# Two transformer blocks on one core: order of the first outputs, lead of the weight splits, places of the waits, and row pitch of two operands

## The chip, the cores and the metric

The kernel is one program on one core of one Trainium2 chip. The metric is its device time in microseconds (us), lower is better. Before the change it takes 1228.34 us, the median of three runs (1228.14 to 1228.73).

## The reference

Everything is float32, one sequence of S = 256 tokens, width D = 1024. Written short:

```
block 1: x += 0.5*swiglu(norm(x), gate0, up0, down0)            # D_FF 2816
         q,k,v,g = norm(x) @ w_in                               # 5888 columns: 12 dilated-window heads, 8 MoBA heads, 2 gates
         x += (sigmoid(ga)*(y_a @ w_up_a) + sigmoid(gb)*(y_b @ w_up_b)) @ w_out
         x += 0.5*swiglu(norm(x), gate1, up1, down1);  x = norm(x)
block 2: (sh, sc, g) x 4 = silu(c) @ ada_w + ada_b              # modulation
         layer 0: x += g1*sliding_window_sink_attention(h(x));  x += g2*swiglu(h(x), gate2, up2, down2)
         layer 1: x += g1*stick_breaking_attention(h(x));       x += g2*swiglu(h(x), gate3, up3, down3)
norm(x) = x * rsqrt(mean(x*x) + 1e-6) * gain;   h(x) = norm(x)*(1+sc) + sh
```

(w_in has 3*768 + 3*512 + 2*1024 columns.) The work is almost all weight matmuls: 2992 weight tiles of 128x128, each against the 256 tokens.

## The kernel before, in words

**Data.** x lies transposed, as KD = 8 slices of 128 features by 256 tokens. To keep float32 accuracy every operand is split in a high and a low part of a reduced float32 format: a weight w into `whi` and `wlo`, the normed input h into `hhi` and `hlo` (8 slices, k = 0..7), the hidden of a swiglu into `hidhi` and `hidlo` (22 slices). Each weight tile takes three matmuls of 256 columns: whi with hhi (L471), whi with hlo (L472), wlo with hhi (L475). Where the input has a shift (mix2, ffn2, mix3, ffn3), two more columns carry it: 258 columns. A row of `hhi` and `hlo` has S + 2 elements (1032 bytes), one of `hidhi` and `hidlo` 256 (1024 bytes).

**Stages.** In order: ffn0, down0, mix1, up, wout, ffn1, down1, mix2, wo2, ffn2, down2, mix3, wo3, ffn3, down3. `TILES` lists all tiles in order; 8 of them are a chunk of 512 KB (374 chunks), and the time that TensorE takes for one chunk is called a tick. "Tick 5.4" of a stage is tile 4 of its chunk 5. `by_output(outs, K, group, late)` sets a stage's order: the first `group` outputs do all k but the last `late` one after another, then the last k together; the rest go output by output. `heads_order` does it for wo2 and wo3, with k from LATE = 5 on left to the end.

**Queues.** SyncE loads chunks into 6 raw buffers (and 96 rows of `ada`, 512 KB each, between them). ScalarE (ACT) copies a chunk to `whi` (L1517, `hi(upto)`), VectorE (DVE) subtracts to `wlo` (L958, `lo(upto)`); both have rings of RING = 7. In tick t of a stage DVE makes `lo` up to chunk t + 2 and ACT `hi` up to t + 3. DVE also makes the modulation from `ada` (L964). Every engine works strictly in the order of the code, which is written by tick: the small operations of a tick stand before or after its `lo` or `hi`.

**Norms.** A stage doesn't wait for its norm: it multiplies raw x by the gain, and the result is scaled later by Rb, the reciprocal root of the mean square. ACT squares x (`squares`), GpSimd (POOL) adds the 8 slices (L1903), TensorE adds over partitions (`sums`, L501), DVE and ACT make the root (`variance`, `estimate`, `inverse`), TensorE spreads it (`spread`, L509), ACT copies it to Rb (`roots`, L1560).

**Residuals.** DVE adds a finished output m to x (`residual`, L984), then ACT makes hhi[m] (`operand_hi`, L1533) and DVE hlo[m] (`operand_lo`, L975) for the next stage. DOWN_AT, WOUT_AT and WO2_AT say in which tick; what is missing there comes after the loop.

**Attention.** TensorE does the head work between weight tiles: `scores`, transposes of the probabilities (`keys_first`, L560), products with v (`outputs`, L567). In mix1 `SETS` and `PAIRS` give the tick of each group of heads; `turns(jp, tick)` begins with `e.wait_ge(norm1, ...)`, ahead of its first `upto(tick, ...)`. mix2 (rotary keys, sinks) goes through one pair of heads a tick, mix3 one in three ticks; there `behind` (L897) does the cumulative sum, after DVE's and ACT's softplus.

Of the kernel before, what the change touches and what calls it, by code (L numbers as in the profile page):

```python
# [28 lines left out]
LATE = 5  # L29
# [34 lines left out]
def mix1_order():  # L64
    order = by_output(MIX1_OUTS[:6], KD, 3, 1)
# [14 lines left out]
def heads_order(name):  # L80

    order = [((name, m), k) for k in range(LATE) for m in range(KD - 2)]
    order += [((name, m), k) for k in range(LATE) for m in (KD - 2, KD - 1)]
# [140 lines left out]
def two_blocks(nc: bass.Bass, x_in, stream, ada, con_in, c_in, pos_in, out):  # L224
    with ExitStack() as ctx:
# [13 lines left out]
        hhi = sb("hhi", [P, KD, S + 2], F32R)  # L239
        hlo = sb("hlo", [P, KD, S + 2], F32R)  # L240
# [161 lines left out]
        def _(e):  # L402
# [5 lines left out]
            for s, (kind, n) in enumerate(SEQ):  # L408
# [35 lines left out]
        def _(e):  # L444
# [67 lines left out]
            def ffn(n):  # L512
# [4 lines left out]
                def begin(o, new):  # L517
                    w, f = o
                    up = w[0] == "u"
                    if new:  # L520
# [4 lines left out]
                        if n > 1 and f < 2:  # L525
# [45 lines left out]
            def mix1():  # L571
# [56 lines left out]
                def turns(jp, tick):  # L628
                    e.wait_ge(norm1, 2 * jp + 2)
# [15 lines left out]
                upto(3, 2)  # L645
# [80 lines left out]
            def mix2():  # L726
# [84 lines left out]
                upto(3, 2)  # L811
# [29 lines left out]
            def mix3():  # L841
# [104 lines left out]
        def _(e):  # L946
# [1076 lines left out]
```

## Time and profile before

| | us |
|---|---|
| median of 3 runs | 1228.34 |
| time of the profiled execution | 1227.34 |
| its span (first to last instruction) | 1225.4 |
| TensorE matmul busy (9696 matmuls) | 1181.0 (96%) |
| DVE busy | 905.2 (74%) |
| ACT busy | 637.2 (52%) |
| POOL busy | 106.9 (9%) |
| DMA | 251.92 MB, 206 GB/s mean |

Matmuls are pipelined, so the busy time of one (279 to 291 ns) overlaps the next; a matmul's price is the distance from start to start. Times are of one profiled execution; "idle before" is how long an engine stood before an instruction, with what released it.

### The profile page before, as it was taken

What the parts mean: (1) busy time and instruction counts of PE and PEld (TensorE: products, weight loads), DVE (VectorE), ACT (ScalarE), POOL (GpSimd) and SP (SyncE); (2) the same over time, 40 slices, a digit from 0 to 9 for tenths busy, and PEclk for the clock granted to TensorE, in tenths of its full rate; (3) what the DMA queues carried; (4) which work ended last, traced back from release to release, by engine and by line L of the source; (5) the groups of instructions that cost most, each with busy time, mean ns of one, the idle gap of its engine ahead of it and who ended that gap; (6) DMA issues with size and microseconds to landing.
All of it is one profiled execution on the core that took longest, in us unless ns stands there. A gap on an engine that the chain in (4) does not pass through costs nothing.

```text
span 1225.4 us, 23733 instructions
## 1 busy us (share of the span) xinstructions
PE 1181.0 (96%) x9696; PEld 1149.3 (94%) x9696; DVE 905.2 (74%) x1589; ACT 637.2 (52%) x1053; POOL 106.9 (9%) x146
## 2 busy tenths in 40 slices
PE   6999999988999999999999999999999998999999
PEld 5999999977889999999987889999998888999999
DVE  4689988465367899997979778888657777666643
ACT  5554555434464654444656654545447785544541
POOL 1000002022100100000455210000100001000000
PEclk8999999989999999999999989999999999999999
DMA  6597878542236588989742357778653434565552
GB/s 247 180 316 250 316 301 311 187 155 82 91 121 180 184 297 302 310 305 347 268 142 74 104 172 259 260 257 299 230 166 113 138 121 146 167 190 187 176 187 86
DMA packets 70524, 251.92 MB, mean 206 GB/s; under 512 B 7824, under 2 KB 9616, under 8 KB 70416
## 3 DMA queue, kind: packets, MB, share of 16 engines
q1 hardware_dynamic: 70416, 250.41, 61.0%
q8 instruction: 77, 1.26, 0.4%
q14 instruction: 31, 0.25, 0.1%
HBM read 249.33 MB, written 1.05 MB: 204 GB/s over the span
## 4 chain that ended last, share of the span: by engine, by line
PE 83%; DVE 11%; ACT 2%; issue 2%; POOL 1%; DMA 1%; SPq 0%; POOLq 0%; DVEq 0%; ACTq 0%
PE ps L471 25%; PE ps L475 25%; PE ps L472 25%; DVE wlo L958 2%; PE ps L567 1%; PE ps L462 1%; ACT s L1747 1%; PE ps L560 1%; PE ps L465 1%; PE ps L466 1%; DVE hlo L975 1%; PE ps L601 1%; DMA raw<-w_stream 1%; PE ps L897 1%; DVE s L1349 1%
## 5 line engine op out<-in xcount | busy, mean ns | idle before, releaser
L471 PE MATMUL ps<-hhi,whi 128*128 128x256 f32 (+1 forms) x1968 | 568.1, 289 | 7.2 <-DVE hlo L975 6.2
L475 PE MATMUL ps<-hhi,wlo 128*128 128x256 f32 (+1 forms) x1968 | 558.2, 284 | 1.0 <-DVE wlo L958 0.8
L472 PE MATMUL ps<-hlo,whi 128*128 128x256 f32 (+1 forms) x1968 | 557.8, 283 | 0.0
L958 DVE TENSOR_TENSOR wlo<-raw,whi 128x1024 fp32r<-128x1024 f32 x373 | 454.3, 1223 | 23.9 <-ACT whi L1517 23.2
L1517 ACT ACTIVATE whi<-raw 128x1024 fp32r<-128x1024 f32 x373 | 386.1, 1048 | 61.6 <-DMA raw<-w_stream 39.3
L471 PEld LDWEIGHTS ps<-hhi,whi 128*128 128x128 f32 x1968 | 374.7, 190 | 15.6 <-issue 14.3
L475 PEld LDWEIGHTS ps<-hhi,wlo 128*128 128x128 f32 x1968 | 374.8, 190 | 1.7 <-DVE wlo L958 1.3
L472 PEld LDWEIGHTS ps<-hlo,whi 128*128 128x128 f32 x1968 | 375.7, 191 | 0.3
L475 PE MATMUL ps<-hidhi,wlo 128*128 128x256 f32 x704 | 196.1, 279 | 0.0
L471 PE MATMUL ps<-hidhi,whi 128*128 128x256 f32 x704 | 196.1, 279 | 0.0
L472 PE MATMUL ps<-hidlo,whi 128*128 128x256 f32 x704 | 196.1, 279 | 0.0
L471 PEld LDWEIGHTS ps<-hidhi,whi 128*128 128x128 f32 x704 | 133.6, 190 | 0.0
L472 PEld LDWEIGHTS ps<-hidlo,whi 128*128 128x128 f32 x704 | 132.1, 188 | 0.0
L475 PEld LDWEIGHTS ps<-hidhi,wlo 128*128 128x128 f32 x704 | 132.1, 188 | 0.0
L964 DVE CUSTOM_DVE_ANT_0 raw<-raw,cond,vx 128x1024 f32<-128x1024 f32 x96 | 126.6, 1319 | 0.0
L1903 POOL TENSOR_TENSOR ss<-sq,ss 128x256 f32<-128x256 f32 x56 | 47.3, 851 | 792.8 <-ACT sq L1540 790.0
L1060 DVE TENSOR_TENSOR gu<-ps,Rb 128x512 f32<-128x512 f32 x88 | 60.4, 686 | 30.5 <-PE ps L475 30.4
L1573 ACT ACTIVATE sg<-gu,bcol 128x256 f32<-128x256 f32 x44 | 22.4, 510 | 105.7 <-DVE gu L1060 105.7
L1577 ACT ACTIVATE hidhi<-hidf 128x256 fp32r<-128x256 f32 x88 | 36.7, 419 | 47.0 <-DVE hidf L1068 33.0
L1573 ACT ACTIVATE sg<-gu 128x256 f32<-128x256 f32 x44 | 18.4, 418 | 80.3 <-DVE gu L1060 80.3
L1059 DVE COPY bcol<-ps 128x2 f32<-128x2 f32 x44 | 7.0, 160 | 61.5 <-PE ps L475 61.4
L984 DVE SCALAR_TENSOR_TENSOR vx<-ps,mod,vx 128x256 f32<-128x256 f32 x32 | 14.0, 477 | 49.1 <-PE ps L475 49.1
(216 smaller groups left out, 1257.1 us busy)
## 6 DMA issues: line engine op xcount, KB each, us to landing
raw<-w_stream SPq DMA_DIRECT2D x373, 512.0 KB, 4.5
raw<-ada_in SPq DMA_DIRECT2D x96, 512.0 KB, 4.8
out_dram<-vx SPq DMA_DIRECT2D x8, 128.0 KB, 2.4
con<-con_in SPq DMA_DIRECT2D x1, 962.0 KB, 6.1
raw<-w_stream SPq DMA_DIRECT2D x2, 256.0 KB, 3.4
vx<-x_in SPq DMA_DIRECT2D x2, 256.0 KB, 6.2
cond<-c_in SPq DMA_DIRECT2D x1, 512.0 KB, 4.4
vx<-x_in SPq DMA_DIRECT2D x3, 128.0 KB, 4.1
```

The source lines that it names most:

```text
L462: e.matmul(b, x_hi, wh, start=kt == 0 and tt == 0, stop=False, skip_group_check=True)
L471: e.matmul(bank, wh, r_hi, start=i == FIRST[o] and not shared, stop=False, skip_group_check=True)
L472: e.matmul(bank, wh, r_lo, start=False, stop=False, skip_group_check=True)
L475: mm = e.matmul(bank, wl, r_hi, start=False, stop=i == LAST[o], skip_group_check=True)
L958: e.tensor_tensor(wlo[:, n % RING, :], raw[:, slot, :], whi[:, n % RING, :].bitcast(F32), ALU.subtract).then_inc(lo_done, 1)
L964: e.tensor_tensor_reduce(raw[:, slot, :], raw[:, slot, :], cond[:], 1.0, v("adab", n), ALU.mult, ALU.add, mod[:, layer, j:j + 1]).then_inc ...
L984: e.scalar_tensor_tensor(x[:, m, :], ps[:, b, o:o + S], coef(r, m), x[:, m, :], ALU.mult, ALU.add).then_inc(x_new, 1)
L1060: e.tensor_tensor(gu[:, b, :, :], ps[:, p:p + 2, 0:S], Rb[:].unsqueeze(1).to_broadcast([P, 2, S]), ALU.mult).then_inc(gu_scaled, 1)
L1517: e.activation(whi[:, n % RING, :], raw[:, s % RAW, :], ACT.Copy).then_inc(hi_done, 1)
L1573: e.activation(sg[:, b, :], gu[:, b, 0, :], ACT.Silu, bias=bcol[:, b, 0:1] if n > 1 else 0.0).then_inc(sg_done, 1)
L1577: e.activation(hidhi[:, f, :], hidf[:, f % 3, :], ACT.Copy).then_inc(hid_hi, 1)
L1903: e.tensor_tensor(ss[:, i, :], sq[:, i, m % 2, :], ss[:, i, :], ALU.add).then_inc(ss_done, 1)
```

## The change

Eight edits in one diff:

1. `by_output` is called with late = KD in all stages: the first 3 or 4 outputs go k by k together. `heads_order` goes over k 0..2, then 3..5 (LATE = 6), each for outputs 0..3 and then 4..7; k = 6 and 7 come last, output by output.
2. `lo` runs to t + 3 (was t + 2) and `hi` to t + 4 (was t + 3) in all stages.
3. Norms: in the swiglu stages `sums` at tick 2.4 (was 1.4) and `spread` at 4.0 (was 3.2), in ffn0 at 5.0 and 6.4; `inverse` stands right behind `variance`, ahead of `lo`. In the mixers `spread` is at 2.4. In ffn0 ACT makes squares 3 to 7 between its first splits. `SCALE_AT` gives the ticks in which gate and up are scaled.
4. mix1: `turns` first runs `upto(tick)`, then waits, and starts 3 ticks after the scores (was 2); the second set and the pairs start 1 to 2 ticks later; the pair scores go ahead of the pair's turns. BIASES is 4 (was 5).
5. mix2: the key's root and `keys` stand ahead of `lo`. mix3: `outputs`, `behind` and `turn_values` come 3 to 4 tiles later.
6. wo2 and wo3: one pair of outputs is added in tick 7, the other three pairs after the loop, each with its own operands and squares.
7. Banks: FFN_OFF (0, 2, 2, 2) and down1, down2, down3 in bank m. ffn2 waits for 2 residuals instead of up to 8.
8. Rows of hhi, hlo, hidhi and hidlo are HS = S + 16 elements, 1088 bytes. x parts 3 to 5 are loaded one chunk later, behind chunks 1 to 3.

```diff
-LATE = 5
+LATE = 6
+HS = S + 16
-    return by_output(outs, KD, 4, 1 if n else KD)
+    return by_output(outs, KD, 4, KD)
...
-    order = [((name, m), k) for k in range(LATE) for m in range(KD - 2)]
-    order += [((name, m), k) for k in range(LATE) for m in (KD - 2, KD - 1)]
+    halves = range(0, KD // 2), range(KD // 2, KD)
+    order = [((name, m), k) for ks in (range(0, 3), range(3, LATE)) for half in halves for k in ks for m in half]
     return order + [((name, m), k) for m in range(KD) for k in range(LATE, KD)]
...
-SETS = [(17, 0, 0), (19, 0, 1), (23, 1, 0), (25, 1, 1)]
-PAIRS = [(29, 0), (31, 1), (33, 2), (35, 3)]
-BIASES = 5
+SETS = [(17, 0, 0), (19, 0, 1), (24, 1, 0), (26, 1, 1)]
+PAIRS = [(31, 0), (33, 1), (35, 2), (37, 3)]
+BIASES = 4
-WO2_AT = {6: (0, 1), 7: (2, 3)}
+WO2_AT = {7: (0, 1)}
-FFN_OFF = (0, 2, 0, 0)
+FFN_OFF = (0, 2, 2, 2)
+SCALE_AT = [{**first, **{t: (t // 2 - 1,) for t in range(10, 44, 2)}} for first in ({7: (0, 1), 8: (2,), 9: (3,)}, {5: (0, 1), 6: (2,), 8: (3,)})]
...
-        hhi = sb("hhi", [P, KD, S + 2], F32R)
-        hlo = sb("hlo", [P, KD, S + 2], F32R)
+        hhi = sb("hhi", [P, KD, HS], F32R)
+        hlo = sb("hlo", [P, KD, HS], F32R)
-            hidhi = sb("hidhi", [P, KF, S], F32R, scope)
-            hidlo = sb("hidlo", [P, KF, S], F32R, scope)
+            hidhi = sb("hidhi", [P, KF, HS], F32R, scope)[:, :, 0:S]
+            hidlo = sb("hidlo", [P, KF, HS], F32R, scope)[:, :, 0:S]
...
-                if s < 3:
-                    load_x(s + 3)
-                if s == 3:
+                if 0 < s < 4:
+                    load_x(s + 2)
+                if s == 4:
...  ffn on TensorE
-                            taken = ((4, 6), (8, 8))[f][up] if n == 2 else ((2, 4), (6, 8))[f][up]
-                            e.wait_ge(x_new, (s - 1) * KD + taken)
+                            e.wait_ge(x_new, (s - 1) * KD + 2)
-                tiles(c0 + CH + 4, begin, operand)
+                tiles(c0 + (2 * CH + 4 if n else 5 * CH), begin, operand)
                 sums(s)
-                tiles(c0 + 3 * CH + 2, begin, operand)
+                tiles(c0 + (4 * CH if n else 6 * CH + 4), begin, operand)
                 spread(s)
...  mix1 on TensorE
                 def turns(jp, tick):
+                    upto(tick)
                     e.wait_ge(norm1, 2 * jp + 2)
...
-                        turns(jp, tick + 2)
+                        turns(jp, tick + 3)
...
+                    pair_scores(p)
                     if p:
-                        pair_turns(p - 1, upto, keys_first, outputs, tick)
-                    pair_scores(p)
-                upto(37)
-                pair_turns(3, upto, keys_first, outputs, 37)
+                        pair_turns(p - 1, upto, keys_first, outputs, tick, 3)
+                pair_turns(3, upto, keys_first, outputs, 39, 6)
...  mix3 on TensorE
-                        upto(3 * i + 1, 6)
+                        upto(3 * i + 2, 2)
                         outputs(i - 2)
-                        upto(3 * i + 3, 2)
+                        upto(3 * i + 3, 6)
                         behind(i - 1)
-                        upto(3 * i + 3, 4)
+                        upto(3 * i + 3, 7)
                         turn_values(i)
...  DVE, every stage (ACT alike, + 3 to + 4)
-                    lo(c0 + t + 2)
+                    lo(c0 + t + 3)
...  DVE, mix2
+                    if t == 5:
+                        keys()
+                    if t == 4:
+                        roots(0, stk, None)
+                        key_roots()
-                    lo(c0 + t + 2)
-                    if t == 4:
-                        roots(0, stk, None)
-                        key_roots()
-                    if t == 5:
-                        keys()
+                    lo(c0 + t + 3)
-                residuals(3, (4, 5, 6, 7), c0 + 20)
+                for ms in ((2, 3), (4, 5), (6, 7)):
+                    residuals(3, ms, c0 + 20)
+                lo(c0 + 21)
...  ACT, ffn0
-            for m in range(KD):
+            for m in range(3):
                 squares(0, m)
+                    if n == 0 and t < 3:
+                        for m in ((3,), (4, 5), (6, 7))[t]:
+                            squares(0, m)
```

## Rows read from the trace of the kernel before

**Rows 1.** Page: busy time of each engine.

```profile
PE 1181.0 (96%) x9696; PEld 1149.3 (94%) x9696; DVE 905.2 (74%) x1589; ACT 637.2 (52%) x1053; POOL 106.9 (9%) x146
```

**Rows 2.** Waits of TensorE: engine, line, releaser, us in total, times, longest.

```profile
PE ps L462 <- DVE sA L1192: 9.9, 2, 5.0
PE ps L501 <- POOL ss L1903: 8.3, 1, 8.3
PE ps L471 <- DVE hlo L975: 6.2, 4, 3.0
PE ps L897 <- DVE zr L1435: 3.7, 7, 1.0
PE ps L560 <- DVE s L1349: 2.4, 2, 1.8
PE ps L763 <- DVE kT L1326: 2.1, 1, 2.1
PE ps L560 <- ACT vt L1802: 1.3, 1, 1.3
PE ps L471 <- DVE o2lo L1354: 1.0, 1, 1.0
PE ps L471 <- ACT mghi L1700: 1.0, 1, 1.0
```

**Rows 3.** Windows over the half-clock stretches: us, busy (x) PE, PEld, DVE, ACT, POOL, clock.

```profile
16.40:26.70 10.30, 5.59 (x26) 5.59 (x27) 3.30 (x8) 4.91 (x9) 3.94 (x6) 0.50 0.49 186
269.00:275.90 6.90, 4.69 (x22) 4.69 (x23) 3.10 (x5) 1.49 (x3) 3.83 (x3) 0.51 0.53 154
303.10:310.00 6.90, 4.38 (x20) 4.38 (x21) 3.41 (x5) 1.81 (x3) 4.15 (x3) 0.51 0.46 152
709.30:716.20 6.90, 6.09 (x27) 5.79 (x27) 4.43 (x5) 2.73 (x4) 2.58 (x4) 0.51 0.43 131
1033.60:1037.10 3.50, 3.29 (x16) 3.04 (x16) 2.38 (x3) 1.56 (x2) 0.82 (x2) 0.51 0.11 42
```

**Rows 4.** Windows, L471 alone: us, PE busy (xtiles), PEld; ffn1, down1, down2, ffn3.

```profile
440.00:540.00 100.00, 78.69 (x281) 52.81 (x280) 1.00 0.88 300
552.00:611.80 59.80, 48.54 (x176) 32.92 (x176) 1.00 0.85 306
838.70:900.80 62.10, 49.40 (x176) 33.72 (x176) 1.00 0.74 258
1080.00:1160.00 80.00, 62.87 (x224) 42.07 (x224) 1.00 0.58 184
```

**Rows 5.** Timeline of ACT and POOL at the start: start, us, what.

```profile
19.35 0.42 ACT L1540 ACTIVATE sq<-vx 128x256 f32<-128x256 f32 x1 [0.45 <-POOL ss L1903]
14.70 6.36 POOL L1903 TENSOR_TENSOR ss<-sq,ss 128x256 f32<-128x256 f32 x7 [14.27 <-ACT sq L1540]
```

**Rows 6.** Windows of all engines, columns as rows 3: middle of mix2, and ffn1.

```profile
672.00:678.00 6.00, 6.00 (x51) 5.12 (x50) 5.55 (x22) 3.95 (x13) 4.89 (x8) 1.00 0.27 79
425.20:552.00 126.80, 126.80 (x1065) 126.75 (x1064) 116.08 (x174) 62.81 (x93) 1.16 (x2) 1.00 0.88 300
```

**Rows 7.** Timeline of DVE from the end of wo2 into ffn2.

```profile
701.36 1.36 DVE L975 SCALAR_TENSOR_TENSOR hlo<-vx,gmod,hhi 128x256 fp32r<-128x256 f32 x2
704.57 1.83 DVE L975 SCALAR_TENSOR_TENSOR hlo<-vx,gmod,hhi 128x256 fp32r<-128x256 f32 x2
706.32 1.65 DVE L984 SCALAR_TENSOR_TENSOR vx<-ps,mod,vx 128x256 f32<-128x256 f32 x4
707.89 1.21 DVE L958 TENSOR_TENSOR wlo<-raw,whi 128x1024 fp32r<-128x1024 f32 x1
709.02 3.58 DVE L975 SCALAR_TENSOR_TENSOR hlo<-vx,gmod,hhi 128x256 fp32r<-128x256 f32 x4
```

**Rows 8.** Timeline of POOL over the same stretch.

```profile
708.92 3.40 POOL L1903 TENSOR_TENSOR ss<-sq,ss 128x256 f32<-128x256 f32 x4 [2.80 <-ACT sq L1540]
```

**Rows 9.** Groups of L471 by form: xcount, busy us, mean ns, idle before.

```profile
L471 PE MATMUL ps<-hhi,whi 128*128 128x256 f32 x992 | 284.4, 287 | 1.0 <-ACT whi L1517 1.0
L471 PE MATMUL ps<-hhi,whi 128*128 128x258 f32 x976 | 283.7, 291 | 6.2 <-DVE hlo L975 6.2
L471 PE MATMUL ps<-hidhi,whi 128*128 128x256 f32 x704 | 196.1, 279 | 0.0
```

More of the change, by code:

```diff
@@ L80, in heads_order @@
 def heads_order(name):
-    order = [((name, m), k) for k in range(LATE) for m in range(KD - 2)]
-    order += [((name, m), k) for k in range(LATE) for m in (KD - 2, KD - 1)]
+    halves = range(0, KD // 2), range(KD // 2, KD)
+    order = [((name, m), k) for ks in (range(0, 3), range(3, LATE)) for half in halves for k in ks for m in half]
     return order + [((name, m), k) for m in range(KD) for k in range(LATE, KD)]
 STAGES = (("ffn0", ffn_order(0)), ("down0", down_order(0)), ("mix1", mix1_order()), ("up", up_order()),
-          ("wout", by_output([("wout", m) for m in range(KD)], KD, 4, 1)),
-          ("ffn1", ffn_order(1)), ("down1", down_order(1)), ("mix2", by_output(MIX2_OUTS, KD, 3, 1)), ("wo2", heads_order("wo2")),
-          ("ffn2", ffn_order(2)), ("down2", down_order(2)), ("mix3", by_output(MIX3_OUTS, KD, 3, 1)), ("wo3", heads_order("wo3")),
+          ("wout", by_output([("wout", m) for m in range(KD)], KD, 4, KD)),
+          ("ffn1", ffn_order(1)), ("down1", down_order(1)), ("mix2", by_output(MIX2_OUTS, KD, 3, KD)), ("wo2", heads_order("wo2")),
+          ("ffn2", ffn_order(2)), ("down2", down_order(2)), ("mix3", by_output(MIX3_OUTS, KD, 3, KD)), ("wo3", heads_order("wo3")),
           ("ffn3", ffn_order(3)), ("down3", down_order(3)))
@@ L665, in pair_turns @@
                 for hh in range(2):
-                    upto(tick, 2 * hh)
+                    upto(tick, tile + 2 * hh)
                     keys_first(12 + 2 * p + hh, sA[:, hh, p % 2, :])
-                upto(tick, 4)
+                upto(tick, tile + 4)
                 outputs(6 + p, 6 + p, 12 + 2 * p + 2, True, True)
@@ L731, in begin @@
                     n = MIX2_OUTS.index(o)
-                    if new and n in (0, 1):
-                        e.wait_ge(x_new, 2 * KD + n + 1)
+                    if new and n < 3:
+                        e.wait_ge(x_new, 2 * KD + (1, 2, 6)[n])
                     if new and n == 5:
@@ L1239, in mix1 @@
                             normed(q, hh)
-                        if hh and t == tick + 4:
+                        if hh and t == tick + 5:
                             heads_lo(jp)
@@ L1476, in mix3 @@
                         shift_lo(3)
-                residuals(5, (4, 5, 6, 7), c0 + 34)
+                for ms in ((2, 3), (4, 5), (6, 7)):
+                    residuals(5, ms, c0 + 34)
+                lo(c0 + 35)
             e.memset(dg[:], 0.0).then_inc(zeroed, 1)
@@ L1667, in mix1 @@
                     for q, (tick, jp, hh) in enumerate(SETS):
-                        if hh and t == tick + 2:
+                        if hh and t == tick + 3:
                             for n in range(4):
                                 turned(6 * jp + n)
-                        if hh and t == tick + 3:
+                        if hh and t == tick + 4:
                             for n in range(4, 6):
@@ L1674, in mix1 @@
                             heads_hi(jp, 3 * jp + 3)
[L1675 to L1681 removed]
+                    hi(c0 + t + 4)
+                    if t == 2:
                         roots(1)
@@ L1686, in mix1 @@
                     for tick, p in PAIRS:
+                        if t == tick + 2:
+                            turned(12 + 2 * p)
+                            turned(12 + 2 * p + 1)
+                    for tick, p in PAIRS:
                         if t == tick:
                             pair_exps(p)
+                        if t == tick + 2:
+                            heads_hi(2 + p, 6 + p + 1)
                     if t == 40:
@@ L1790, in mix2 @@
                         operands(4, WO2_AT[t - 10])
-                operands(4, (4, 5, 6, 7))
-                hi(c0 + 21)
+                for ms in ((2, 3), (4, 5), (6, 7)):
+                    operands(4, ms)
+                hi(c0 + 22)
             def mix3():
@@ L1859, in mix3 @@
                         operands(6, WO2_AT[t - 24])
-                operands(6, (4, 5, 6, 7))
-                hi(c0 + 35)
+                for ms in ((2, 3), (4, 5), (6, 7)):
+                    operands(6, ms)
+                hi(c0 + 36)
             exp_ln_table()
```

121 lines of the change are left out of this document (57 added, 64 removed).

## The prediction, before the result was known

> **What bounds the kernel now.** I read the page's busy times first. TensorE is busy 1181.0 of 1225.4 us, DVE 74%, ACT 52%, POOL 9% [rows 1]. So time goes only where TensorE stands still, runs at the lower clock, or needs less for a matmul. Three views price these: its waits, the windows with a granted clock near 0.5, and windows in which only L471 is counted, one per weight tile.
>
> Standing still: the waits listed come to 36 us, of which 24.4 us are three places: two waits for mix1's probabilities (9.9), one for POOL's sum at the start (8.3), four for hlo (6.2) [rows 2].
>
> Lower clock: after five of these waits the granted clock is 0.5 (1.2 GHz) for a stretch. Work in it takes double. TensorE is busy in them 5.59, 4.69, 4.38, 6.09 and 3.29 us; half of it is lost: 2.8, 2.3, 2.2, 3.0 and 1.6 us, together 12.0 [rows 3].
>
> Price of a tile (three matmuls) at full clock, window by count: 100.0 / 281 = 0.356 us in ffn1 (256 columns), 80.0 / 224 = 0.357 in ffn3 (258 columns), 59.8 / 176 = 0.340 in down1, 62.1 / 176 = 0.353 in down2 [rows 4]. down1 and down2 read the same rows of the same tensors, and still there are two levels, 113 and 118 ns a matmul. No row says what picks one.
>
> **The change part by part.** The sum is made against the profiled execution, 1227.34 us; the median of the runs is 1.0 above it.
>
> *Start (edits 3 and 8).* The wait of 8.3 us ended at 21.1, when POOL's seven adds were done (14.70 + 6.36) [rows 2, 5]. TensorE had stopped at 12.8, after 12 tiles. Now `sums` stands at tile 40, so 28 tiles of 0.357, 10.0 us, lie ahead of it: 22.8. ACT's squares 3 to 7 now have splits of 1.05 us between them, which I let push the last add by about 1 us, to 22: covered, just. x parts behind the chunks make the first operands later; I charge 0.7. DVE's `variance` blocks no `lo` needed: chunks up to 7 are split ahead of it. The wait goes, and with it the low-clock stretch: 8.3 + 2.8 - 1.1 = 10.0. Bounds: 6 (the sum 4 us later) and 11.
>
> *mix1 (edit 4).* TensorE waits for norm1 right behind the scores, though 16 tiles that don't need it come next in its own queue; behind the wait stood everything. The wait now comes after 24 tiles, 8.6 us, more than the 5.0 us of each wait [rows 2]. Gone: 9.9, and 4.5 of low clock. The pairs' waits were small. BIASES 4 makes POOL write two of the second set's three biases only after the first set is softened; the 5.7 us between the sets (16 tiles) hide two adds of POOL's size (0.9 each [rows 5]). Without that cover it would cost 2. I take 14.5, bounds 10 and 15.5.
>
> *wo2 to ffn2, wo3 to ffn3 (edits 1, 6, 7).* Output by output, ffn2 wanted hlo of k = 4 at its fifth tile, 1.4 us in. k by k over four outputs it is wanted after 16 tiles, 5.7 us. DVE's work for a pair of slices: two residuals (1.65 / 4 = 0.41 each) and two hlo (3.58 / 4 = 0.90 each), 2.6 us [rows 7]. TensorE wants a pair each 8 tiles, 2.9 us. From the start of the tail of 16 tiles: first pair finished at 1.4, one split 1.2, four pairs 10.5, so the last at 13.1; wanted at 5.7 + 24 x 0.357 = 14.3. It holds with 1.2 to spare. What is late next: `sums` at tile 20, 12.8, wants the last add of POOL, about 14: 1.2 us in each stage. The next `wlo` (1.21) ends at 14.3, just as chunk 3 is wanted. Gone: 6.2 waits and 4.6 low clock, and 1.0 for o2lo, since k = 7 now comes 7 tiles behind its product. 11.8 - 2.4 = 9.4, bounds 4 and 12. New early use of outputs 4 to 7's banks adds a wait on `du2` in wo2 (TensorE alone stands behind it, under 1 us; inside the bounds).
>
> The hlo of those rows is slow when POOL adds: 1.36 for two while POOL has nothing, 3.58 for four during its four adds [rows 7, 8]. The Trainium skill, "SBUF — State Buffer", section "Who interferes with whom", says that a DVE instruction with two SBUF inputs and a GpSimd one that reads SBUF exclude each other. The trace agrees (0.68 and 0.90 us each). It speaks against edit 6, which puts POOL's adds among all pairs; I have used the slow value for all eight slices. By the fast one the tail would have 1.8 us more room, and the sum stays.
>
> *mix3 (edit 5).* `behind` waited 3.7 us in seven places, at most 1.0; it comes 4 tiles, 1.4 us, later. The transpose of v waited 1.3 and comes 3 tiles later [rows 2]. I take 4.5 of 5.0. `outputs` is moved by as much, and its users have 13 tiles. Bounds 2 and 5.
>
> *mix2 (edit 5), wout (edit 1).* The wait for kT, 2.1, shrinks, as a `lo` (1.21 [rows 7]) no longer stands before it. But in the middle of mix2 DVE is busy 5.55 of 6.0 us [rows 6], so what TensorE gains early it waits for later; the 2.4 us for s stay. 1.5, bounds 0 and 4. In wout k = 6 is wanted 18 tiles later: 1.0.
>
> *Splits one chunk ahead (edit 2).* TensorE's waits for splits are 2 us in all, at the start. An operation of tick t on DVE now stands behind a split of t + 3, which needs a ring slot that TensorE left four ticks before: free by then. 0, bounds -2 and 2.
>
> Waits and clock together: 10.0 + 14.5 + 9.4 + 4.5 + 1.5 + 1.0 = 41.
>
> *Pitch of 1088 bytes (edit 8).* 1968 tiles read hhi and hlo: 992 with 256 columns, 976 with 258 [rows 9], at 0.356 and 0.357. 704 read hidhi and hidlo, half at 0.340, half at 0.353. The stages with a pitch of 1032 are at neither of the two levels; those with a pitch of 1024 are. With 1088 every row starts at the same place of a 64-byte grid, as with 1024, so I expect the two levels in all stages. All at the lower: 992 x 16 ns + 976 x 15 + 352 x 13 = 35 us saved. All at the upper: 3 + 2 saved, 4.6 lost in down0 and down1: 0. All at 0.357: 7 us lost. Both levels occur now about equally often, so I take the middle with some allowance for the worst, 15. Speed of the others is enough: at 0.340 ffn1 would want 352 x 0.340 = 119.7 us, DVE has 116.1 us of work in it [rows 6].
>
> In all 56: 1227.3 - 56 + 1.0 = 1172.
>
> The Trainium skill, same page and section, says that TensorE never waits on anyone in reading SBUF. By that rule the pitch could change nothing between engines; the two levels in down1 and down2 show that something besides the operand's row sets the price. No run here yet tells what.
>
> **Rivals.**
> - *The lower level everywhere.* For it: down1 holds 113 ns through 176 tiles. Against: down2 and down3 don't. 1228 - 41 - 35 = 1152. Chance 0.17.
> - *The pitch does nothing.* For it: the levels differ at equal pitch, so pitch may not be what matters. 1228 - 41 = 1187. Chance 0.18.
> - *The waits come back.* DVE is at 92% in ffn1 and in mid-mix2 [rows 6]; the `sums` in the swiglu stages and the bank waits are new. If half of the 41 returns and the pitch gives 5: 1228 - 20 - 5 = 1203. Chance 0.10.
> - *Slower.* One mechanism: rows at a pitch of 1088 collide with weight loads, and all 2672 tiles cost more. It decides from 41 / 2672 = 15 ns a tile, 5 ns a matmul, that is from 124 ns a matmul. The mean matmul with hhi, at a pitch of 1032, shows 287 and 291 ns, one with hidhi, at 1024, 279 [rows 9]: 4% between pitches, which speaks against. At 10 ns a matmul: 1228 - 41 + 80 = 1267. Chance 0.05.
>
> **How the numbers follow.** The forecast, waits gone and a mixture of levels, has 0.50, with 1160 to 1185 as its own range. Range for 8 in 10: from a little under the first rival to the third, 1146 to 1200. No change is within 0.2%, about what a measurement tells. Faster holds in all cases but the last, and I leave some for a wait I have overlooked that is long enough to lower the clock again: faster 0.91, same 0.02, slower 0.07.
>
> **What would show it.** TensorE's waits: no L501 <- POOL at the start, no L462 <- sA, hlo waits under 1 us; L501 <- ss about 1 us each in ffn2 and ffn3. Windows: clock 1.0 between 20 us and the end, except perhaps around mix2. L471 counts per window: 0.340 or 0.353 in ffn stages. I am wrong on the waits if DVE's or POOL's rows end the waits of TensorE with over 20 us in sum; wrong on the pitch if ffn1 still takes 0.356, or over 0.36, a tile.

## The result, and the profile after

The changed kernel takes 1188.32 us, the median of 4 runs (1187.18 to 1188.91); beside it the kernel before took 1228.38 (1228.14 to 1228.73). The ratio is 0.9673, interval 0.9656 to 0.9689: 40 us, 3.3%, faster. Predicted were 1172 and a range of 1146 to 1200. It is faster, and inside the range, but outside the forecast's own 1160 to 1185: 16 us less gain than foreseen. The profiled execution took 1188.88 us, span 1186.9.

Busy times, answering to [rows 1]:

```profile
PE 1172.6 (99%) x9696; PEld 1143.9 (96%) x9696; DVE 904.9 (76%) x1589; ACT 634.7 (53%) x1053; POOL 109.2 (9%) x146
```

Waits of TensorE, answering to [rows 2] (engine, line, releaser, us in total, times, longest). L471 of before is L474 now, L501 is L504, L462 L465, L560 L562.

```profile
PE ps L504 <- POOL ss L1915: 3.7, 3, 2.4
PE ps L562 <- DVE s L1350: 2.4, 2, 1.9
PE ps L931 <- DVE dg L1482: 1.4, 1, 1.4
PE ps L474 <- ACT whi L1520: 1.1, 1, 1.1
PE ps L478 <- DVE wlo L961: 0.7, 1, 0.7
PE ps L766 <- DVE kT L1327: 0.6, 1, 0.6
```

No wait on sA, on hlo, on zr or on vt is left. The wait at the start has shrunk from 8.3 to 2.4 us; the other two of L504 are those at the beginning of ffn2 and ffn3. The half-clock stretches are down from five to two, answering to [rows 3]: behind the sums of ffn0 and in the middle of mix2. They lose 1.7 us each; before it was 12.0 in all.

```profile
26.30:29.70 3.40, 3.40 (x18) 3.40 (x17) 3.23 (x7) 1.93 (x3) 0.00 (x0) 0.50 0.45 153
627.10:630.50 3.40, 3.40 (x17) 3.17 (x19) 2.62 (x12) 2.50 (x11) 1.66 (x3) 0.51 0.55 159
```

The windows that count weight tiles, L474 alone, answer to [rows 4]: ffn1, down1, down2, ffn3, and wout as a fifth (us, PE busy (x tiles), PEld, clock, DMA share, GB/s).

```profile
440.00:540.00 100.00, 78.82 (x281) 52.57 (x281) 1.00 0.89 306
529.80:591.90 62.10, 49.19 (x176) 32.91 (x177) 1.00 0.85 306
812.00:874.10 62.10, 49.22 (x176) 32.91 (x177) 1.00 0.73 254
1030.00:1110.00 80.00, 63.12 (x224) 42.31 (x224) 1.00 0.60 184
380.80:403.30 22.50, 17.82 (x64) 11.92 (x65) 1.00 0.60 182
```

(The first window reaches a little into down1.) ffn1 still takes 0.356 us a tile and ffn3 0.357; down1 went from 59.8 to 62.1 us for its 176 tiles. So the waits went as foreseen, and the pitch didn't give the time that it was to give; the next section shows that it took some.

Stage by stage, in us, from the start of a stage's first weight matmul to the start of its last (ffn0 with what lies ahead of it; a wait between two stages is in neither):

| | before | after | after, old pitches |
|---|---|---|---|
| start and ffn0 | 146.7 | 138.8 | 138.1 |
| down0 / down1 | 59.8 / 59.8 | 62.1 / 62.1 | 59.8 / 59.8 |
| mix1 | 178.5 | 162.7 | 162.7 |
| up / wout | 16.2 / 23.6 | 16.9 / 22.5 | 16.2 / 21.6 |
| ffn1 | 126.6 | 126.3 | 126.6 |
| mix2 / wo2 | 52.7 / 39.9 | 51.3 / 39.3 | 51.3 / 39.3 |
| ffn2 / ffn3 | 132.9 / 132.7 | 128.2 / 127.9 | 127.8 / 127.8 |
| down2 / down3 | 62.1 / 62.1 | 62.1 / 62.1 | 62.1 / 62.1 |
| mix3 / wo3 | 98.2 / 28.2 | 91.4 / 28.1 | 91.4 / 27.7 |

### The profile page after: what moved, and what is told of

Read it like the earlier page. It is cut to its first block, busy times and chain, and to the rows that moved or that the text cites. A ratio compares the mean times of both kernels' runs of the same rounds, so it can differ in the third digit from the quotient of the medians.

```text
span 1186.9 us, 23734 instructions
## 1 busy us (share of the span) xinstructions
PE 1172.6 (99%) x9696; PEld 1143.9 (96%) x9696; DVE 904.9 (76%) x1589; ACT 634.7 (53%) x1053; POOL 109.2 (9%) x146
## 4 chain that ended last, share of the span: by engine, by line
PE 91%; DVE 4%; ACT 2%; POOL 1%; issue 1%; DMA 1%; SPq 0%; POOLq 0%; ACTq 0%; DVEq 0%
PE ps L474 28%; PE ps L475 28%; PE ps L478 27%; PE ps L569 1%; POOL ss L1915 1%; PE ps L562 1%; DVE wlo L961 1%; PE ps L465 1%; PE ps L469 1%; PE ps L468 1%; ACT s L1755 1%; PE ps L603 1%; DVE hlo L978 1%; DMA vx<-x_in 1%; PE ps L885 1%
## 5 line engine op out<-in xcount | busy, mean ns | idle before, releaser
L474 PE MATMUL ps<-hhi,whi 128*128 128x256 f32 (+1 forms) x1968 | 565.2, 287 | 1.1 <-ACT whi L1520 1.1
L478 PE MATMUL ps<-hhi,wlo 128*128 128x256 f32 (+1 forms) x1968 | 552.7, 281 | 0.9 <-DVE wlo L961 0.7
L961 DVE TENSOR_TENSOR wlo<-raw,whi 128x1024 fp32r<-128x1024 f32 x373 | 456.6, 1231 | 28.6 <-ACT whi L1520 28.2
L474 PEld LDWEIGHTS ps<-hhi,whi 128*128 128x128 f32 x1968 | 372.5, 189 | 8.9 <-issue 6.5
L478 PEld LDWEIGHTS ps<-hhi,wlo 128*128 128x128 f32 x1968 | 374.8, 190 | 1.4 <-DVE wlo L961 0.9
L478 PE MATMUL ps<-hidhi,wlo 128*128 128x256 f32 x704 | 197.4, 280 | 0.0
L474 PE MATMUL ps<-hidhi,whi 128*128 128x256 f32 x704 | 197.0, 280 | 0.0
L478 PEld LDWEIGHTS ps<-hidhi,wlo 128*128 128x128 f32 x704 | 132.2, 188 | 0.0
L474 PEld LDWEIGHTS ps<-hidhi,whi 128*128 128x128 f32 x704 | 132.0, 187 | 0.0
L1915 POOL TENSOR_TENSOR ss<-sq,ss 128x256 f32<-128x256 f32 x56 | 53.9, 969 | 765.7 <-ACT sq L1543 763.1
```

The lines of the kernel that those rows point to most:

```text
L474: e.matmul(bank, wh, r_hi, start=i == FIRST[o] and not shared, stop=False, skip_group_check=True)
L478: mm = e.matmul(bank, wl, r_hi, start=False, stop=i == LAST[o], skip_group_check=True)
L961: e.tensor_tensor(wlo[:, n % RING, :], raw[:, slot, :], whi[:, n % RING, :].bitcast(F32), ALU.subtract).then_inc(lo_done, 1)
L1915: e.tensor_tensor(ss[:, i, :], sq[:, i, m % 2, :], ss[:, i, :], ALU.add).then_inc(ss_done, 1)
```

## The experiments

Twelve kernels ran. Each time is the median of 4 or 5 runs, except one that is said to be a single run, and each ratio is to runs of the kernel before on the same chip.

### The pitch, undone and alone

The changed kernel with the old pitches:

```diff
-hhi = sb("hhi", [P, KD, HS], F32R)                      # hlo too
+hhi = sb("hhi", [P, KD, S + 2], F32R)
-hidhi = sb("hidhi", [P, KF, HS], F32R, scope)[:, :, 0:S] # hidlo too
+hidhi = sb("hidhi", [P, KF, S], F32R, scope)
```

> The changed kernel with the row pitches of before: hhi and hlo 1032 bytes, hidhi and hidlo 1024 (BIASES stays 4). Theory P, the pitch of 1088 is what holds down0, down1 and up at 118 ns a matmul: with 1024 they can go back to 113 (4.6 us for down0 and down1, 0.7 for up), ffn0, mix1 and ffn1 go from 118.9 to 119.2 (+0.9 us in all): 1184 us. Theory C, the level is picked by how TensorE enters a stage and not by the pitch: 1188 us with down0 and down1 still at 118, or any mixture. Rival, the pitch gained time as the prediction had it: 1195 us or more.

Measured: 1181.46 us (1180.91 to 1182.30), ratio 0.9623 (0.9610 to 0.9636), 6.9 us less than the changed kernel, with no overlap of the runs. Its windows over down0, up, wout, ffn1, down1 and down2:

```profile
138.10:197.90 59.80, 48.56 (x176) 32.97 (x177) 1.00 0.86 312
360.70:377.00 16.30, 13.24 (x48) 8.96 (x49) 1.00 0.59 182
377.00:398.70 21.70, 17.64 (x64) 11.95 (x65) 1.00 0.55 187
410.00:510.00 100.00, 78.59 (x279) 52.48 (x279) 1.00 0.89 305
525.50:585.30 59.80, 48.55 (x176) 32.97 (x177) 1.00 0.85 311
805.10:867.20 62.10, 49.43 (x176) 33.70 (x177) 1.00 0.74 254
```

And the kernel before with the new pitch, and with BIASES 4 to make room for it:

```diff
-hhi = sb("hhi", [P, KD, S + 2], F32R)   # hlo, hidhi, hidlo alike
+hhi = sb("hhi", [P, KD, HS], F32R)
-BIASES = 5
+BIASES = 4
```

> The kernel before with only the pitch of 1088 bytes in the four tensors (BIASES 4 for room). Theory P: down0, down1 and up at 118 ns instead of 113 (+5.3 us), 256-column stages 0.3 ns a matmul less (-0.9): 1232 to 1233 us. Theory C: no fixed direction, 1228 +- 5. Prediction's step (15 us saved): 1213 us.

Measured: 1233.19 us (1232.30 to 1234.52), ratio 1.0045 (1.0032 to 1.0058). Its windows over down0, over ffn1 and over down2:

```profile
146.80:208.90 62.10, 49.23 (x176) 32.91 (x177) 1.00 0.84 307
440.00:540.00 100.00, 78.74 (x282) 52.62 (x281) 1.00 0.87 303
845.80:907.90 62.10, 49.18 (x176) 32.94 (x176) 1.00 0.74 260
```

Both ways agree: 1088 bytes cost 4.7 us without the other edits and 6.9 with them. down0 and down1 lose 2.3 us each, up 0.6, and in the changed kernel wout 0.9; the tiles of ffn0 and ffn1 win 0.3 each. (In the table above ffn0 is longer after the change than with the old pitches, by 0.7. That isn't the pitch, see "The sums of ffn0, later".) So the edits of order and waits alone are worth 1228.4 - 1181.5 = 46.9 us.

### mix1's wait, one line

The kernel before with the first line of the new `turns`:

```diff
 def turns(jp, tick):
+    upto(tick)
     e.wait_ge(norm1, 2 * jp + 2)
```

> The kernel before with one line more: turns() in mix1 first runs its tiles up to its tick, then waits for norm1. 16 tiles (5.7 us) come between scores and wait, each wait was 5.0 us idle. Theory, the wait's place was its whole cost, and the low clock came from the idle: both go, 9.9 + 4.5 us, 1214 us, and no window of mix1 has a clock under 1.0. Rival, the wait moves to the next consumer (DVE or ACT late after it): half is kept, 1221 us.

Measured: 1214.18 us (1212.75 to 1215.00), ratio 0.9887 (0.9874 to 0.9901), 14.3 us less than the 1228.46 beside it; mix1 went from 178.5 to 164.4. The wait on sA at L462 (9.9 us) is gone, and the clock is full throughout; what is left of waits in this stretch are five short ones. The window over mix1, and the waits of the same stretch:

```profile
185.00:350.00 165.00, 163.71 (x1346) 153.65 (x1345) 102.27 (x222) 79.34 (x143) 26.29 (x24) 1.00 0.53 172
```

```profile
PE ps L560 <- DVE sA L1215: 0.7, 3, 0.2
PE ps L560 <- ACT pT L1653: 0.6, 2, 0.3
```

16 tiles that TensorE had in its own queue, moved ahead of a wait, are over a third of the whole gain of 40.

### First outputs k by k, undone

The changed kernel with `late` = 1 again where it was 1 (the down stages and up keep their order in the change too, although its list says "in all stages"):

```diff
-    return by_output(outs, KD, 4, KD)              # mix1, wout, mix2 and mix3 alike
+    return by_output(outs, KD, 4, 1 if n else KD)
```

> The changed kernel with the old order at the head of every stage but ffn0 (the first 3 or 4 outputs run through k = 0 to 6 each, k = 7 together). Theory, k by k is what covers DVE's residual and hlo chain: TensorE wants hlo[k] of ffn2 and ffn3 within its first 7 tiles (2.5 us), DVE delivers a pair each 2.6 us, so waits of 3 us or more come back in both, with a low clock behind, and 1 us in wout: 1188 + 10 to 16 = 1198 to 1204 us. Rival, the new pairwise end of wo2 and wo3 does it alone: 1188 to 1191 us.

Measured: 1194.30 us (1192.51 to 1195.34), ratio 0.9722 (0.9706 to 0.9737), 6.0 us more than the changed kernel. That is between the two theories, and neither holds in full: ffn2 takes 132.7 (128.2), ffn3 130.1 (127.9), wout 23.1 (22.5). The waits on hlo are back, and behind the one in ffn2 the clock drops to a mean of 0.84 for 15 us:

```profile
PE ps L474 <- DVE hlo L978: 4.6, 4, 1.2
PE ps L474 <- ACT whi L1520: 1.8, 1, 1.8
```

```profile
690.00:705.00 15.00, 15.00 (x108) 14.95 (x107) 11.84 (x21) 6.96 (x11) 1.17 (x1) 0.84 0.69 225
```

So of the 9.5 us that ffn2 and ffn3 gained together, 6.7 come from the order of the first outputs, with the other edits in place; the other edits there are left with 2.8, which no run separates.

### The lead of the splits, undone

The changed kernel with the old pitches and one chunk less of lead:

```diff
-    lo(c0 + t + 3)          # every stage, and what follows the loops
+    lo(c0 + t + 2)
-    hi(c0 + t + 4)
+    hi(c0 + t + 3)
```

> The changed kernel with the old pitches (1181.5 us) and the old lead: lo to t + 2, hi to t + 3. Theory of the prediction (the lead is worth nothing): 1179.5 to 1183.5. Rival (the lead is what covers DVE's bursts between wo2 and ffn2, in mix1 and at the start): waits on wlo and hlo return, 5 to 12 us, with low clock behind them: 1187 to 1195.

Measured: 1181.42 us (1181.10 to 1182.80), against 1181.46 with the lead. TensorE waits 3.2 us on wlo in four places instead of 0.9 in two, but less elsewhere: start and ffn0 take 1.1 us less than with the lead (137.0 for 138.1), ffn3 0.9 more (128.7 for 127.8). In sum the lead is worth nothing, as the prediction had it, but by a balance of small terms and not because no wait depends on it:

```profile
PE ps L478 <- DVE wlo L961: 3.2, 4, 1.4
```

### What sets the level of a tile

Next the pitch of the stages of 256 columns was set to 1024 bytes for all four operands (one buffer with two views, 1024 for the stages up to ffn1, 1032 from mix2 on).

```diff
-hhi = sb("hhi", [P, KD, S + 2], F32R)    # hlo alike
+hbuf = sb("hhi", [P, KD * (S + 2)], F32R)
+early = hbuf[:, 0:KD * S].rearrange("p (k c) -> p k c", k=KD)
+late = hbuf[:].rearrange("p (k c) -> p k c", k=KD)
```

> The changed kernel with hidhi and hidlo at a pitch of 1024 bytes again, and hhi and hlo at 1024 in the stages of 256 columns (ffn0, down0, mix1, up, wout, ffn1), at 1032 in those of 258. The run with 1032 throughout took 1181.5 us; ffn0, mix1 and ffn1 showed 119.2 ns a matmul there, 3216 matmuls in all. Theory (the pitch, not the stage, keeps them off the two levels): the same stages fall to 113.3 ns (19.0 us less, 1162.5) or to 117.8 (4.5 us less, 1177). Rival (the stages with hhi and hlo cost more for another reason, since down0 and wout read other operands or stand elsewhere): 119.2 stays, 1181.5.

Measured: 1185.91 us (1185.10 to 1186.63), ratio 0.9661 (0.9647 to 0.9675). Neither theory's sum came out. ffn0 and ffn1 did fall to 0.353, as half of the first said, 1.3 us in ffn1; but down0 and down1, whose rows are the same 1024 bytes as before, rose from 59.8 to 62.1, and up and wout from 0.340 to 0.353 too. The windows over ffn1 and down1:

```profile
410.00:510.00 100.00, 78.31 (x282) 52.75 (x281) 1.00 0.90 307
528.30:590.40 62.10, 49.39 (x176) 33.72 (x176) 1.00 0.84 305
```

Nothing of down1's own was changed against the kernel with the old pitches; what changed is the pitch of the stages ahead of it, and the buffers kept their sizes. The same in the changed kernel with only hidhi and hidlo at 1024 again:

```diff
-hidhi = sb("hidhi", [P, KF, HS], F32R, scope)[:, :, 0:S]   # hidlo alike
+hidhi = sb("hidhi", [P, KF, S], F32R, scope)
```

> The changed kernel with hidhi and hidlo at 1024 bytes again, hhi and hlo left at 1088. Theory C (a stage at 1024 takes the level that it comes in with: up and wout, whose operands nobody touched, went from 113.3 to 117.8 with the change): down0 and down1 come in from ffn stages at 1088 and stay at 117.8: 1187 to 1189. Rival P (the operand's own pitch sets the level: 1024 behind 256 columns is 113.3): down0 and down1 at 113.3, 4.6 us less: 1183.7.

Measured: 1187.97 us (1186.76 to 1188.60), ratio 0.9683 (0.9670 to 0.9697). Theory C, not P. The windows over down0 and up (the change never touched up's operands):

```profile
137.90:200.00 62.10, 49.08 (x176) 32.99 (x177) 1.00 0.85 308
362.80:379.70 16.90, 13.36 (x48) 8.96 (x49) 1.00 0.56 185
```

And the kernel of 1024 bytes with 256 columns instead of 258 in the late stages, at 1024 too. It leaves out the shift of the modulation, so it doesn't compute the reference's result, and it serves for its times alone:

```diff
-    cols = S + 2 if n > 1 else S
+    cols = S                        # ffn2, ffn3; mix2 and mix3 alike
```

> The kernel with pitch 1024 where it can be, and the matmuls of mix2, ffn2, mix3 and ffn3 with 256 columns at pitch 1024 instead of 258 at 1032: it leaves out the shift of the modulation (the two extra columns). Theory (a stage of 258 columns leaves down2 and down3 on the upper level, and costs 119.4 itself by its pitch): down2 and down3 fall to 113.3 (1056 matmuls, 4.7 us), the four stages (2928 matmuls) to 113.3 or 117.8 (18 or 4.9 us): 10 to 23 us less than the kernel with pitch 1024. Rival (down2 and down3 are on the upper level for another reason): they stay at 117.8, and only the four stages gain.

Measured: 1182.77 us (1178.09 to 1183.46), 3.1 us less than the kernel it was made from. down2 and down3 stay at 62.1 us: 258 columns don't decide them. ffn3 fell to 0.353 a tile, but ffn2, the same code on the same rows, rose to 0.360. One pitch, one width, two levels. One of its four runs, 1178.09, was 4.5 us faster than the next, about two times the 2.3 us that 176 tiles gain from 0.353 to 0.340; and of nine runs of the kernel before on one chip two took 1225.8 and 1226.0 us, seven 1228.1 to 1228.8. So a level may also change between two executions of the same kernel. There is a trace of only one execution of each, and no run shows it.

### Thirty cuts: the level is a phase

If the level is no property of a stage's rows, something carries it. One kernel disturbs TensorE 30 times: every 32 tiles the first matmul of a tile is made as two.

```diff
-e.matmul(bank, wh, r_hi, start=..., stop=False)
+for a, b in ((0, SPLIT[i]), (SPLIT[i], S)) if i in SPLIT else ((0, None),):
+    e.matmul(bank[:, a:b], wh, r_hi[:, a:b], start=..., stop=False)
```

> The kernel with hhi and hlo at 1024 in the stages of 256 columns and hidhi and hidlo at 1024 (1185.9 us, 117.8 ns in all of them), with 30 single interruptions: in ffn0, down0, ffn1 and down1 the first matmul of every 32nd tile is cut into two, of c and 256 - c columns, c from 2 to 254. Nothing else changes between two of them. Theory C (the level is a phase in which TensorE falls into step, kept until something disturbs it): after some of the 30 the level steps from 117.8 to 113.3 or to 120.0 and stays there until the next. Rival P (the level is a property of the stage's operands): each cut costs its own 0.1 to 0.2 us and the level stays at 117.8 throughout.

One run, 1185.61 us. Windows that count the third matmul of a tile (L486, which no cut touches), each in a stretch without a cut: in ffn0 ahead of the cut at column 240 and behind it, behind the cut at 2; in down0 ahead of the first cut, behind the cut at 128, and behind the cut at 32.

```profile
83.40:94.00 10.60, 8.40 (x31) 5.63 (x30) 1.00 0.91 307
94.90:105.70 10.80, 8.55 (x31) 5.63 (x30) 1.00 0.76 248
118.20:128.80 10.60, 8.41 (x31) 5.63 (x31) 1.00 0.95 339
140.90:151.50 10.60, 8.43 (x31) 5.63 (x31) 1.00 0.92 307
152.50:162.70 10.20, 8.27 (x31) 5.63 (x30) 1.00 1.01 407
174.60:184.80 10.20, 8.28 (x30) 5.63 (x31) 1.00 0.76 266
```

The window lengths are 30 tiles at 0.353, 0.360 and 0.340 (the counts round at the edges): the same stage on the same rows runs at two levels, and one short disturbance switches it. From the starts of the matmuls, all stretches but two (the norms of ffn0 and ffn1 fall in them) are level from the second tile behind the cut to the next cut: of the 20 in ffn0 and ffn1, 7 are at 0.360 and 13 at 0.353, none at 0.340; of the 10 in down0 and down1, 8 are at 0.340 and 2 at 0.353. The first stretches of down0 and down1, ahead of any cut, are at 0.353. A cut costs about 0.1 us (tiles of 0.45 to 0.47). up and wout behind them, without any cut, came out at 0.340 this time. Theory C is shown for rows of 1024 bytes. It happens without a cut too: in the kernel with the one line in `turns`, down1 went from 0.340 to 0.353 at its tile 120, behind a single tile of 0.390, and stayed there. (The kernel before has a tile of 0.380 at the same place, and stays at 0.340.) What makes one cut end high and another low isn't shown: cuts at 16 and at 8 columns, with the same way into them, differ in down1.

### Using it

The changed kernel with the old pitches and one cut each in down2 and down3:

```diff
+SPLIT = {2043: 128, 2827: 128}     # tile 11 of down2 and of down3, and the loop above
```

> The changed kernel with the old pitches (1181.5 us) and two cuts: in down2 and down3 the first matmul of tile 11 is made as two of 128 columns. Both stages ran at 117.8 ns a matmul in every kernel so far. In the study of 30 cuts, 8 of the 10 in down0 and down1 left the stage at 113.3, each cut cost about 0.1 us. Theory C (a kept phase): 164 tiles of each stage fall from 0.353 to 0.340 us, 2.2 us a stage, less 0.1 for the cut: 4.2 us less in all, 1177.3; if only one of the two cuts falls well, 1179.4. Rival (down2 and down3 have the upper level from their tensors' place or the state left by 258 columns, not from a phase): 1181.7.

Measured: 1177.28 us (1176.20 to 1177.90), ratio 0.9597 (0.9583 to 0.9612), as theory C had it (1177.3), and the best of all. The 1181.5 that it is set against was measured on another chip; by the ratios, each to the kernel before on its own chip, the cuts gain 3.2 us (0.9597 for 0.9623), and that the medians agree to 0.1 us is in part luck. The traces show the gain in its place: down2 and down3 take 60.0 us each for 62.1. The first two windows of this kernel lie behind the cuts in down2 and down3 (L480), and the third is the stretch of down2 without a cut (L478 of the kernel without cuts):

```profile
809.30:860.30 51.00, 41.41 (x150) 28.13 (x151) 1.00 0.74 266
1116.00:1167.00 51.00, 41.39 (x151) 28.16 (x150) 1.00 0.43 146
```

```profile
809.30:860.30 51.00, 40.59 (x145) 27.03 (x144) 1.00 0.75 261
```

### The sums of ffn0, later

POOL's seven adds ran from 15.20 to 25.01 after the change. Two kernels put `sums` 8 tiles later, one at pitch 1024, one with the old pitches.

```diff
-tiles(c0 + (2 * CH + 4 if n else 5 * CH), begin, operand)
+tiles(c0 + (2 * CH + 4 if n else 6 * CH), begin, operand)
-tiles(c0 + (4 * CH if n else 6 * CH + 4), begin, operand)
+tiles(c0 + (4 * CH if n else 7 * CH), begin, operand)
```

> The kernel with pitch 1024 where it can be, and in ffn0 the sums 8 tiles and the spread 4 tiles later (chunk 6.0 and 7.0). In the changed kernel the sums waited 2.6 us for POOL's seventh add, and 3.4 us at half clock followed. Theory (only the end of the adds, drawn out by DVE's splits, sets the wait): 8 tiles of 0.34 to 0.357 us are 2.7 to 2.9 us, the wait goes and the low clock with it, 4.0 to 4.4 us less than without this edit. Rival (the low clock comes anyway, or DVE's root, which is later too, makes the splits late): 2 us less or nothing.

Measured: 1185.53 us (1185.43 to 1186.59), 0.4 less than without the edit; the two spreads overlap. The clock was 0.79 over 24 to 32 us without it and is 1.00 with it:

```profile
24.00:32.00 8.00, 6.46 (x41) 6.47 (x42) 4.29 (x9) 2.81 (x5) 1.48 (x1) 0.79 0.64 203
```

```profile
24.00:32.00 8.00, 7.53 (x62) 7.13 (x62) 5.56 (x12) 4.67 (x8) 1.52 (x1) 1.00 0.61 180
```

21 matmuls more in 8 us, 2.5 us. But ffn0 ran at 0.360 a tile in this trace, not at 0.353, and its 340 tiles took 2.3 us back: another phase. The edit didn't bring it. The 24 tiles up to tile 39, ahead of the sums' old place and of the new, took 8.64 us with it and 8.48 without. They took 8.64 as well in the kernel with 256 columns in the late stages, whose TensorE code is the same up to there; that kernel went to 0.353 behind its wait for the sums. So the same code entered ffn0 at two levels, and where the stop was taken away the level stayed. At the old pitches, where the undisturbed part of ffn0 is at 0.3575 in every trace:

> The changed kernel with the old pitches (1181.5 us) and in ffn0 the sums 8 tiles, the spread 4 tiles later. With pitch 1024 in ffn0 the same edit took away the wait of 2.6 us and the low clock behind it, but the stage went from 117.8 to 120.0 ns a matmul and gave 2.3 us back. Theory (the level is drawn anew by an interruption only where rows stand at 1024; at 1032 ffn0 showed 119.2 in every kernel): ffn0 stays at 119.2 and down0 at 113.3, so the whole 4 us show: 1177.5. Rival (the later norm itself costs, or the levels of the stages behind change): 1180 to 1184.

Measured: 1180.92 us (1179.18 to 1181.74), ratio 0.9625 (0.9612 to 0.9639) against 0.9623 (0.9610 to 0.9636) without it: no difference. The theory's 4 us were a mistake in the base: with the old pitches the profile shows 1.5 us of waits on POOL in three places, none over 0.6, and 1.1 in two with the edit. Why the first of them is 2.4 us in the changed kernel and 0.6 with the old pitches, the windows over 11 to 17 us tell (all engines, columns as in [rows 3]), the old pitches first and the changed kernel below:

```profile
11.00:17.00 6.00, 5.30 (x31) 5.10 (x31) 5.01 (x8) 5.70 (x11) 1.17 (x2) 0.72 1.04 412
```

```profile
11.00:17.00 6.00, 5.71 (x48) 5.72 (x49) 4.87 (x8) 5.91 (x12) 1.66 (x2) 1.00 1.04 413
```

With the old pitches the half clock came here, before the sums, and TensorE was through with tile 39 at 24.6 us; in the changed kernel it was at 22.4, and POOL's last add ended at 25.5 and 25.0. TensorE lost the time either ahead of the sums or in front of them and behind. It isn't the pitch that decides which: the run with late = 1, whose start and rows are those of the changed kernel, has the early low clock (0.72 over the same window) and a wait of 0.7. What brings the low clock early in one execution and not in another is open.

## Why the prediction was right and wrong

Set against the kernel with the old pitches, where nothing but order and waits changed:

- *Start: 10.0 predicted, 8.7 measured (7.9 in the changed kernel).* The wait of 8.3 us went as said. The term that was too small is the end of POOL's adds: the prediction had it 1 us later, at 22, and it came 4 us later, at 25.0, with a wait of 2.4 us that it had as "covered, just". The seven adds, 6.36 us in [rows 5], took 9.81:

```profile
15.20 9.81 POOL L1915 TENSOR_TENSOR ss<-sq,ss 128x256 f32<-128x256 f32 x7 [14.77 <-ACT sq L1543]
```

Both numbers hold pauses between the adds. A window over a single add gives 0.74 without a split of DVE beside it, and 1.53 with one; four of the seven took 1.52 to 1.72, and before the change, with no split beside them, six took 0.72 or 0.73:

```profile
20.00:20.85 0.85, 0.74 (x1) 1.00 1.09 323
18.30:20.00 1.70, 1.53 (x1) 1.00 0.99 366
```

DVE's splits beside them, 1.21 in [rows 7], took 1.23 to 1.52:

```profile
16.41 1.23 DVE L961 TENSOR_TENSOR wlo<-raw,whi 128x1024 fp32r<-128x1024 f32 x1 [0.64 <-ACT whi L1520]
17.80 1.52 DVE L961 TENSOR_TENSOR wlo<-raw,whi 128x1024 fp32r<-128x1024 f32 x1 [0.16 <-ACT whi L1520]
21.35 1.41 DVE L961 TENSOR_TENSOR wlo<-raw,whi 128x1024 fp32r<-128x1024 f32 x1 [2.03 <-ACT whi L1520]
```

  The Trainium skill, "SBUF — State Buffer", "Who interferes with whom", has two-input DVE instructions and GpSimd's reads exclude each other. The rows agree (an add and a split that meet cost one of them or both up to 1.0 us more), and the prediction should have used the rule here too: it used it only for hlo. There it misread its row: of the two hlo in the 1.36 of [rows 7] "while POOL has nothing", the second met an add of POOL at 701.56. Alone an hlo takes 0.40, from start to start, and not 0.68.
- *mix1: 14.5 predicted, 15.8 measured*, of which the one line in `turns` is 14.3. Right. The trace shows no wait of TensorE on a bias, but BIASES 4 has no run of its own.
- *wo2 to ffn2, wo3 to ffn3: 9.4 predicted; 0.6 + 5.1 + 0.5 + 4.9 = 11.1 measured.* Right in mechanism; two waits on POOL's sums came as foreseen, at 0.6 in place of 1.2 each. DVE's tail from the second pair on:

```profile
683.87 0.89 DVE L978 SCALAR_TENSOR_TENSOR hlo<-vx,gmod,hhi 128x256 fp32r<-128x256 f32 x2 [0.18 <-ACT hhi L1536]
685.73 1.77 DVE L978 SCALAR_TENSOR_TENSOR hlo<-vx,gmod,hhi 128x256 fp32r<-128x256 f32 x2 [0.19 <-ACT hhi L1536]
688.48 0.89 DVE L978 SCALAR_TENSOR_TENSOR hlo<-vx,gmod,hhi 128x256 fp32r<-128x256 f32 x2 [0.18 <-ACT hhi L1536]
689.28 4.58 DVE L961 TENSOR_TENSOR wlo<-raw,whi 128x1024 fp32r<-128x1024 f32 x3
```

  The slow price (0.9 an hlo) was paid by one pair of three; the other two ran at 0.45. POOL's last two adds met the first two of the three splits behind them, which took 1.77 and 1.75; the third, alone, took 1.21.
- *mix3: 4.5 predicted, 6.8 measured, mis-sized.* TensorE stood still for 4.5 of its 98.3 us before, and not at all after. The other 2.3 are in busy time, at full clock in both. A stop costs more than its wait: 2.3 us over the 7 stops of this stage, 0.3 each. In one of them 0.45 us stood idle, but 0.73 lay between the start of the matmul ahead of it, at 948.63, and the start of the next, where 0.12 is usual: the matmuls no longer overlap. Edit 5 as a whole makes this difference; no run takes it apart. The window over mix3 before, and after (us, busy (x) of PE, PEld, DVE, ACT, POOL, clock, DMA share, GB/s):

```profile
900.90:999.20 98.30, 93.75 (x750) 87.39 (x749) 71.85 (x149) 72.67 (x134) 0.80 (x1) 1.00 0.41 124
```

```profile
874.20:965.60 91.40, 91.40 (x750) 86.55 (x749) 72.84 (x149) 71.38 (x134) 0.81 (x1) 1.00 0.42 133
```

- *mix2: 1.5 predicted, 1.4 measured; the 2.4 us for s stayed,* as foreseen. *wout: 1.0 predicted, 2.0 measured,* of which 0.8 is the level of its tiles (0.340 for 0.353), which the prediction didn't have. *Splits one chunk ahead: 0 predicted, 0 measured,* as a balance.

The sum of these is 46, predicted were 41. Runs of their own show mix1's wait, the order of the first outputs and the lead; the terms of the start, mix2, mix3 and wout rest on the waits in the traces.

- *Pitch of 1088 bytes: 15 saved predicted, 5 to 7 lost measured. This is the step that failed.* It said: "With 1088 every row starts at the same place of a 64-byte grid, as with 1024, so I expect the two levels in all stages", and "both levels occur now about equally often, so I take the middle". Neither held. ffn0 and ffn1 came to 0.3567, on neither level, for 0.3575; ffn2 and ffn3 stayed at 0.3583; and down0, down1, up and wout, at 0.340 with the old pitches, went to 0.353. The level that a stage at 1024 bytes shows is a phase that it comes into and keeps; the cheap one can be lost by what the stage ahead does. The prediction had the clue, down1 and down2 at two levels with the same rows, drew from it that "something besides the operand's row sets the price", and then still forecast a gain from the row. Its bounds ("All at 0.357: 7 us lost") held the result, though not for its reason: no more than 0.353 was paid in the down stages. (In its sums for the 258-column tiles it has 15 and 2 ns a tile where its rows give 17 and 4, 2 us each time. That changes nothing.)

56 predicted = 41 + 15; 40 measured = 47 - 7. The rival "the pitch does nothing" gave 1187, next to the result, but isn't what happened: two errors, 6 too little from the waits and 7 for a loss that it has as 0, cancel by luck. "The waits come back" fell: the new waits of L504 are 3.7 us in all, and with the old pitches 1.5. Nor did rows of 1088 collide with weight loads in all tiles: the dearest level seen is 120.0 ns, below the 124 of that rival.

## What to carry to other kernels

A wait belongs behind the work that the engine already has in its queue: one line that moved 16 ready tiles ahead of a wait gave 14 of the 47 us that the edits of order and waits are worth. Compare the price of the repeated instruction stage by stage before and after each edit: a stream of equal matmuls can run at several levels, 6% apart, for reasons outside its stage, and an edit of layout should be timed by itself before it is kept; here the bundle hid a loss of 7 us. When a step adds work beside another engine's, use the price that both show when they overlap.

## What the runs showed of the hardware

In the traces of thirteen of these fourteen kernels (all but the one with 30 cuts) the undisturbed part of each ffn and down stage (128x128 weights, 256 or 258 columns, a weight load each) ran at one of a few prices, from start to start of two matmuls, mostly over 120 tiles and more: 113.33, 117.78, 118.89, 119.17, 119.44 and 120.00 ns, at a granted clock of 1.00 (0.340 to 0.360 us a tile). The lowest was seen only with rows at 1024 bytes, in stages that don't read hhi and hlo, and 117.78 was seen there as well. Rows of hhi and hlo at 1024 gave 117.78 or 120.00; at 1032 119.17 with 256 columns and 119.44 with 258, in each trace; at 1088 118.89 with 256 and 119.44 with 258. Rows of hidhi and hidlo at 1088 gave 117.78. Why hhi and hlo never had the lowest is open. Within a stage at 1024 the level can be switched by cutting one matmul in two, and then stays for at least the 32 tiles to the next cut, in down3 for all 164 tiles to the end. The Trainium skill, "TensorE: Matmul & The Clock Gate", "Back-to-back issue gap", gives N / 2.4 + 2.5 ns for an isolated gap, an estimate of 109 ns for 256 columns. Here a weight load goes with each matmul, and no such stage ran below 113.3: the measurement decides. What the phase is between (matmul and weight load, or the reading of rows) no run here tells.
